# A two-layer attention decoder: who turns the later layer's probabilities and gates

## The chip, the core and the metric

The kernel runs on one core of one Trainium2 chip. The metric is the time of one execution in device microseconds (us), median of the runs. Engines are named TensorE (PE in the profile; its weight loads are PEld), VectorE (DVE), ScalarE (ACT), GpSimd (POOL) and SyncE (SP), which only issues transfers and waits.

## What is computed

A residual stream of 256 tokens x 2048 in float32 goes through two layers. Layer A is latent attention with 16 heads. Layer B, the later one, is dilated sliding-window attention with 16 heads of 128 in three groups (dilation 1, 4, 16), which share one key/value projection. What matters of layer B:

```
u = rms_norm(h) @ w_in                   # queries of 3 groups and a gate
for g, dil in enumerate((1, 4, 16)):
    q = rms_norm(q_all[g]); s = q @ k[g].T * scale + alibi    # within the window
    o[g], lse[g] = softmax(s) @ v[g], log-denominator
o = sum over g of o[g] * softmax(lse)[g]
out = h + (o * silu(gate)) @ w_o
```

## The kernel before

All weights are streamed from device memory once, in steps of 128 x 1024 float32 (512 KB), into a ring of four buffers `raw`. To keep float32 accuracy each step is split in two: ScalarE rounds it to a high half (`highs`, L478), VectorE subtracts to get the low half (`lows`, L794), and TensorE multiplies three of the four products of halves (`three`, `project`, L1271): 12 matmuls of 512 columns for a step.

SyncE issues the weight loads in the order of use (`load`, L363). Load n waits until the low half of step n-3 counted from one is made (semaphore `lo_ready`), so that its place in the ring is free. ScalarE makes the high half of step n once TensorE has used step n-4. So the halves are made about three steps ahead of TensorE.

Layer B goes over 8 pairs of heads, 40 weight steps each, and then the output projection of 32 steps. The order of all work is written out by hand. While TensorE projects pair i (a "quarter" s is two steps, 20 of them in a pair), the attention of pair i-1 is woven in after the quarters. A pair has four units (2 heads x 2 tiles of 128 tokens). A unit u goes through four stages, one a quarter (`b_units`): stage 0 at quarter u+2, the scores (`b_score`, L1514 and L1519), VectorE's mask and maximum (`band_mask`), ScalarE's exponential into `prob`; stage 1 at u+3, VectorE's reciprocal and scaled gate (`b_gates`, `band_gate`, L899, into `og`), and on TensorE `band_turn`, which transposes three 128x128 blocks of `prob` and one of `og` into a PSUM bank (L1303); ScalarE copies them to `probT` (L516); stage 2 at u+4, the product with the values (`band_pv`, L1536 and L1540), in PSUM, and VectorE's product with the turned gate (`band_out`, L904); stage 3 at u+5, the split of the result into halves for the output projection. The last pair's attention stands in the output projection, at the steps of `B_LAST_SLOTS`.

Keys and queries are turned by VectorE in 32x32 blocks: 16 instructions for a tensor, from a block row a to a block column b (`b_blocks`, L1180). A 32x32-block transpose turns each block in place; which partitions a block lies in is changed by reading one quarter of the partitions and writing another. For the third query group 8 of 16 stand in quarter 0 and 8 in quarter 1, with a low half between.

Each engine takes its own instructions in the order written; semaphores are the only ties.

Of the kernel before, what the change touches and what calls it, by code (L numbers as in the profile page):

```python
# [107 lines left out]

def b_round(i, k):

    return i * UNITS + (B_ROUND_0 - UNITS) + k


QUAD = P // 4
# [11 lines left out]


B_LAST_SLOTS = [0, 1, 3, 5, 7, 9, 11, 12, 13]


# [27 lines left out]
def build_program(nc, xT, x_later, x_tok, identity, consts, alibis, gains, w_in, w_pe, w_kv, w_gate_first, w_gate, w_q, w_out_a, w_b, w_out_b, out_tok):  # L158
    ctx = ExitStack()
    with ctx:  # L160
# [19 lines left out]
        gain = sb("gain", [P, N_GAINS])  # L180
        k_per = sb("k_per", [P, TILES, ROPE])
        pe_sq = sb("pe_sq", [P, TILES, ROPE])
        pe_ss = sb("pe_ss", [P, TILES])
# [5 lines left out]
        prob = sb("prob", [P, 2, 512])  # L189
        probT = sb("probT", [P, 512])  # L190
        q_ropes = (qT[:, 2 * 512:3 * 512], v[:, 2 * 512:3 * 512])
        og = sb("og", [P, 2, P])
        out = sb("out", [P, 2, P])
        half = sb("half", [P, 1])
# [73 lines left out]

        pe_T = og[0:ROPE].rearrange("p a k -> p (a k)")

# [41 lines left out]
        blocked = sem("blocked")  # L312
        gained = sem("gained")
        rot_step = sem("rot_step")
        pe_T_ready = sem("pe_T_ready")
# [38 lines left out]
        def _(sp):  # L354
# [110 lines left out]
        def _(act):  # L465
# [323 lines left out]
        def _(dve):  # L789
# [104 lines left out]
            def band_gate(U, u, g, gates_so_far):  # L894
# [265 lines left out]
            def b_gates(i, s):  # L1160

                for stage, u in b_units(s):
                    if stage == 1:
                        U = (i - 1) * UNITS + (B_UNIT_0 + u)
                        unit_den(U, u)
                        band_gate(U, u, gate[:, 0, u % 2, (u // 2) * P:(u // 2 + 1) * P], i + GATE_FILLS)

            def b_blocks(f, k, n):

                buf, x = (B_CHAIN_0 + k) % 2, qT if f in (Q01, Q2GATE) else kT  # L1170
                a, b = n // 4, n % 4
                for first, groups, swap in {Q01: [(0, 2, 0)], K01: [(0, 1, 0), (1, 1, 1)], K2V0: [(0, 1, 1)],
                                            Q2GATE: [(0, 1, 0)]}[f]:
                    at = (first + 2 * (f in (K2V0, Q2GATE))) * 2 * SEQ
                    col = QUAD * (a ^ 2 if swap else a)
                    src = rows[a * QUAD:(a + 1) * QUAD, buf, :, first * 2 * P:(first + groups) * 2 * P]\
                        .rearrange("p t (u d) -> p t u d", d=P)[:, :, :, b * QUAD:(b + 1) * QUAD]
                    dst = x[b * QUAD:(b + 1) * QUAD, at:at + groups * 2 * SEQ]\
                        .rearrange("p (u t d) -> p t u d", t=TILES, d=P)[:, :, :, col:col + QUAD]
                    last = nc.vector.transpose(dst, src)  # L1180
                return last

            def b_attend(i, s, par_before):
                if s == 0:
                    b_rows(i - 1, par_before, 3)
                    dve.wait_ge(rows_ready, i * 4 + B_CHAIN_0)
                if s < 2:
                    for n in range(8 * s, 8 * s + 8):
                        last = b_blocks(Q2GATE, 3, n)
                    if s == 1:  # L1190
                        last.then_inc(blocked, 1)
                for stage, u in b_units(s):
# [69 lines left out]
        def _(pe):  # L1262
# [258 lines left out]

            def band_turn(U, u, rnd):

                pe.wait_ge(prob_ready, U + 1)
                pe.wait_ge(og_ready, U + 1)
                turn_rows(rnd, [(prob[:, u % 2, k * P:(k + 1) * P], k * P) for k in range(BAND // P)]
                          + [(og[:, u % 2], BAND)])

            def band_pv(U, B, u, rnd):

                h, t = u // 2, u % 2
                pe.wait_ge(turn_read, rnd + 1)
                pe.wait_ge(out_made, B)
                both = probT[:, 0:BAND].rearrange("p (a k) -> p a k", a=2)
                for tile in range(TILES):
                    nc.tensor.matmul(pv.rearrange("p (a k) -> p a k", a=2), v[:, tile * 768 + h * P:tile * 768 + (h + 1) * P],  # L1536
                                     both[:, :, tile * P:tile * P + HP], start=tile == 0, stop=False, skip_group_check=True)
                for half, first in ((0, SEQ), (1, HP)):
                    col = t * 768 + (1 + half) * 256 + h * P
                    last = nc.tensor.matmul(pv[:, half * HP:(half + 1) * HP], v[:, col:col + P],  # L1540
                                            probT[:, first:first + HP], start=False, stop=True, skip_group_check=True)
                last.then_inc(pv_ready, 1)

            def b_attend(i, s):
                for stage, u in b_units(s):
                    U = (i - 1) * UNITS + (B_UNIT_0 + u)
                    if stage == 2:
                        band_pv(U, (i - 1) * UNITS + u, u, b_round(i, u))
                    if stage == 1:
                        band_turn(U, u, b_round(i, u))  # L1550
# [150 lines left out]
```

## Time and profile before

| | us |
|---|---|
| median of 3 runs | 1403.69 (1403.6 to 1404.28) |
| the profiled execution | 1404.01 |
| span of its instructions | 1402.2 |
| TensorE busy | 1395.2 |
| VectorE busy | 1046.5 |
| ScalarE busy | 706.6 |

The span is the time from the first to the last instruction in one profiled execution; what lies around it, 1.8 us, is start and end. Busy times are of instructions as recorded; matmuls overlap their neighbours, so that TensorE at 99% need not be at its peak. The chain of waits is followed back from the last instruction, at each step to what released it, and so shows what set the end. The granted clock of TensorE is 1.00 (2.4 GHz) in every stretch.

### The profile page before, as it was taken

How to read it: one execution, taken by the hardware profiler on the slowest of the kernel's cores; microseconds unless marked ns; L12 is line 12 of the kernel's file. 1: busy time of each engine (PE TensorE's matmuls, PEld its weight loads, DVE VectorE, ACT ScalarE, POOL GpSimd, SP SyncE). 2: the span in 40 equal slices, each digit the busy share in tenths (PEclk: the TensorE clock that was granted, in tenths of full speed). 3: DMA queues.
4: the chain of work that ended last, by engine and by line, in shares of the span. 5: the costliest groups of instructions: out<-in, count | busy, mean ns of one | idle time of the engine just before them, and what ended most of it. 6: DMA issues, size and time to landing. Idle time of an engine off the chain costs nothing.

```text
span 1402.2 us, 20187 instructions
## 1 busy us (share of the span) xinstructions
PE 1395.2 (99%) x6648; PEld 1169.4 (83%) x6648; DVE 1046.5 (75%) x1969; ACT 706.6 (50%) x1032; POOL 102.5 (7%) x67
## 2 busy tenths in 40 slices
PE   9999999999999999999999999999999999999999
PEld 6888888888888888888888888888888888888887
DVE  6767767747667868877877877887887788789653
ACT  6555555646544544544544454544454445454442
POOL 0101001000010001000101100101010110010000
PEclk9999999999999999999999999999999999999999
DMA  9653544455556545645654654565556456555544
GB/s 355 232 173 125 166 143 142 147 190 179 183 187 203 191 151 180 205 155 180 182 194 149 197 181 163 183 198 167 166 188 189 159 186 194 160 181 190 171 165 150
DMA packets 71233, 252.49 MB, mean 180 GB/s; under 512 B 7904, under 2 KB 8288, under 8 KB 71136
## 3 DMA queue, kind: packets, MB, share of 16 engines
q1 hardware_dynamic: 70704, 249.95, 54.7%
q10 hardware_dynamic: 432, 1.31, 0.3%
q8 instruction: 53, 0.87, 0.2%
q14 instruction: 44, 0.36, 0.1%
HBM read 249.14 MB, written 2.10 MB: 179 GB/s over the span
## 4 chain that ended last, share of the span: by engine, by line
PE 94%; DVE 2%; issue 2%; ACT 1%; DMA 0%; POOL 0%; SPq 0%; DVEq 0%; POOLq 0%
PE acc L1271 85%; PE turn L1303 1%; PE score L1514 1%; PE pv_bank L1536 1%; PE score L1519 1%; PE pv_bank L1540 1%; DVE qT L1180 1%; PE pv_bank L1315 1%; PE score L1411 1%; PE score L1413 1%; DVE w_lo L794 1%; PE turn L1397 0%; DMA raw<-in_w_in 0%; PE og_bank L1323 0%; POOL rms L426 0%
## 5 line engine op out<-in xcount | busy, mean ns | idle before, releaser
L794 DVE TENSOR_TENSOR w_lo<-raw,w_hi 128x1024 fp32r<-128x1024 f32 x463 | 574.2, 1251 | 205.9 <-ACT w_hi L478 196.9
L478 ACT ACTIVATE w_hi<-raw 128x1024 fp32r<-128x1024 f32 x463 | 482.4, 1050 | 397.2 <-PE acc L1271 386.0
L1271 PE MATMUL acc<-w_hi,xa_hi 128*128 128x512 f32 x956 | 378.7, 396 | 0.6 <-DVE w_lo L794 0.4
L1271 PE MATMUL acc<-w_hi,xa_lo 128*128 128x512 f32 x956 | 372.8, 390 | 0.0
L1271 PE MATMUL acc<-w_lo,xa_hi 128*128 128x512 f32 x956 | 372.2, 389 | 0.0
L1271 PE MATMUL acc<-w_hi,xb_hi 128*128 128x512 f32 (+1 forms) x640 | 249.4, 390 | 0.0
L1271 PE MATMUL acc<-w_hi,xb_lo 128*128 128x512 f32 (+1 forms) x640 | 245.9, 384 | 0.0
L1271 PE MATMUL acc<-w_lo,xb_hi 128*128 128x512 f32 (+1 forms) x640 | 245.5, 384 | 0.0
L1271 PEld LDWEIGHTS acc<-w_hi,xa_lo 128*128 128x128 f32 x956 | 179.4, 188 | 37.9
L1271 PEld LDWEIGHTS acc<-w_hi,xa_hi 128*128 128x128 f32 x956 | 179.6, 188 | 37.5 <-issue 1.3
L1271 PEld LDWEIGHTS acc<-w_lo,xa_hi 128*128 128x128 f32 x956 | 179.7, 188 | 35.3
L426 POOL TENSOR_TENSOR rms<-ms,mhalf 128x4 f32<-128x4 f32 (+2 forms) x50 | 73.2, 1465 | 1050.6 <-DVE ms L850 855.4
L1271 PEld LDWEIGHTS acc<-w_hi,xb_lo 128*128 128x128 f32 x640 | 120.1, 188 | 22.7
L1271 PEld LDWEIGHTS acc<-w_lo,xb_hi 128*128 128x128 f32 x640 | 120.3, 188 | 22.1
L1271 PEld LDWEIGHTS acc<-w_hi,xb_hi 128*128 128x128 f32 x640 | 120.2, 188 | 22.0
L1180 DVE STREAM_TRANSPOSE kT<-rows 32x128 f32<-32x128 f32 x384 | 102.2, 288 | 4.5
L1271 PE MATMUL acc<-w_hi,oT_hi 128*128 128x512 f32 x256 | 102.3, 400 | 0.0
L1271 PE MATMUL acc<-w_hi,oT_lo 128*128 128x512 f32 x256 | 100.0, 391 | 0.0
L1271 PE MATMUL acc<-w_lo,oT_hi 128*128 128x512 f32 x256 | 99.7, 390 | 0.0
L1180 DVE STREAM_TRANSPOSE qT<-rows 32x256 f32<-32x256 f32 (+1 forms) x256 | 94.5, 369 | 4.1
L532 ACT ACTIVATE prob<-prob,top_neg 128x128 f32<-128x128 f32 (+1 forms) x64 | 34.3, 537 | 91.3 <-DVE top_neg L891 63.9
L516 ACT ACTIVATE probT<-turn 128x128 f32<-128x128 f32 (+1 forms) x64 | 29.7, 463 | 76.7 <-PE turn L1303 57.2
(178 smaller groups left out, 1061.4 us busy)
## 6 DMA issues: line engine op xcount, KB each, us to landing
raw<-in_w_b SPq DMA_DIRECT2D x320, 512.0 KB, 3.6
raw<-in_w_out_a SPq DMA_DIRECT2D x32, 512.0 KB, 3.3
raw<-in_w_out_b SPq DMA_DIRECT2D x32, 512.0 KB, 3.3
raw<-in_w_gate SPq DMA_DIRECT2D x30, 512.0 KB, 3.6
raw<-in_w_kv SPq DMA_DIRECT2D x16, 512.0 KB, 4.3
raw<-in_w_in SPq DMA_DIRECT2D x15, 512.0 KB, 6.2
raw<-in_w_q SPq DMA_DIRECT2D x16, 384.0 KB, 3.0
res<-in_x_tok SPq DMA_DIRECT2D x4, 512.0 KB, 7.8
```

What stands on the lines that cost most here:

```text
L426: nc.gpsimd.tensor_tensor(rms[:, 0:width], ms[:, 0:width], mhalf[:, 0:width], ALU.pow)\
L478: nc.scalar.activation(w[0][:, s, 0:width], raw[:, s, 0:width], ACT.Copy).then_inc(hi_ready, 1)
L516: last = nc.scalar.activation(dst, turn[:, 0:width], ACT.Copy)
L532: nc.scalar.activation(prob[:, u % 2, 0:width], prob[:, u % 2, 0:width], ACT.Exp, bias=top_neg[:, u:u + 1], accum_out=den[:, u:u + 1])\
L794: nc.vector.tensor_tensor(w[1][:, s, 0:width], raw[:, s, 0:width], w[0][:, s, 0:width].bitcast(F32), ALU.subtract).then_inc(lo_ready, 1)
L1180: last = nc.vector.transpose(dst, src)
L1271: last = nc.tensor.matmul(out, x(a), y(b), start=start and k == 0, stop=stop and k == 2, **more)
L1303: last = nc.tensor.transpose(turn[:, col:col + P], src, ident[:])
L1315: last = nc.tensor.matmul(pv, probT[:, k * P:(k + 1) * P], val, start=k == 0, stop=k == len(values) - 1)
L1411: nc.tensor.matmul(score[:, 0:n], qT[:, par * 512 + at:par * 512 + at + P], kT[:, k_0 + h * SEQ:k_0 + h * SEQ + n], start=True, stop=False)
L1413: nc.tensor.matmul(score[:, 0:n], q_ropes[par][:, at:at + P], kT[:, k_0 + 512:k_0 + 512 + n], start=False, stop=True).then_inc(scored, 1)
L1514: nc.tensor.matmul(score[:, P:P + SEQ], qT[:, h * SEQ + t * P:h * SEQ + (t + 1) * P], kT[:, h * SEQ:(h + 1) * SEQ], start=True, stop=True)
```

## The change

TensorE turns nothing any more in layer B. For each unit VectorE turns the 128 x 512 of `prob` (384 columns of probabilities and 128 of gate, which now stands behind them in the same buffer) in one instruction, each 32x32 block in its place, into a new buffer `bands`, of which there is one. Then SyncE issues 16 transfers within on-chip memory, one for each pair of block row a and block column b, 32 rows of 512 bytes each, which put the blocks into `probTs`, of which there are two. The semaphore `band_moved` counts the landings. VectorE's turn waits until the transfers of the unit before have landed; TensorE's value product waits for those of its own unit. In SyncE's order the transfers of unit u stand behind the load of step 14 + 2u of a pair (behind loads 12, 14, 16 and 18 in the output projection). The value product and `band_out` read the turned data in pieces of 32 columns. ScalarE's copy from PSUM goes.

Beside this: the later layer's loops of SyncE are written out; `b_blocks` turns two groups in one instruction for the first two key groups too (16 instructions instead of 32); the 16 transposes of the third query group all stand in quarter 0, and ScalarE's gain on it in quarter 1 instead of 2; `k_per`, `pe_sq`, `pe_T`, `og` and `out` lie in buffers that are free at the time.

```
+B_MOVES = [2 * (u + 3) + 2 * RING for u in range(UNITS)]
+B_LAST_MOVES = [B_LAST_SLOTS[u + 3] - 1 + 2 * RING for u in range(UNITS)]
...
+        bands = sb("bands", [P, 512])
...
+        probTs = sb("probTs", [P, 2, 512])
+        probT = probTs[:, 0]
...
+        og = prob[:, :, BAND:BAND + P]
...
# SyncE
-            with sp.Fori(0, PAIRS) as i:
+            def band_move(B, u):
+                sp.wait_ge(band_turned, B + 1)
+                if not isinstance(B, int) or B >= 2:
+                    sp.wait_ge(out_made, B - 1)
+                for a in range(4):
+                    for b in range(4):
+                        sp.dma_start(probTs[b * QUAD:(b + 1) * QUAD, u % 2, a * P:(a + 1) * P],
+                                     bands[a * QUAD:(a + 1) * QUAD, b * P:(b + 1) * P]).then_inc(band_moved, 16)
+            def b_pair(i, attend):
                 for s in range(B_STEPS):
                     load((i, B_STEPS), B_0 + s, w_b[i, s], STEP)
-            with sp.Fori(0, OUT_STEPS // 8) as j:
-                for q in range(8):
-                    load((j, 8), OUT_B_0 + q, w_out_b[j, q], STEP)
+                    if attend and s in B_MOVES:
+                        u = B_MOVES.index(s)
+                        band_move((i - 1) * UNITS + u, u)
...
+            for k in range(OUT_STEPS):
+                load(OUT_B_0 + k, OUT_B_0 + k, w_out_b[k // 8, k % 8], STEP)
+                if k in B_LAST_MOVES:
+                    u = B_LAST_MOVES.index(k)
+                    band_move((PAIRS - 1) * UNITS + u, u)
...
# ScalarE
-                if s == 2:
+                if s == 1:
                     act.wait_ge(blocked, (i - 1) * 4 + 4)
                     gain_of(qT, 2, q_gain)
...
-                    if stage == 1:
-                        if u:
-                            act.wait_ge(out_made, (i - 1) * UNITS + u)
-                        unit_turned(b_round(i, u), u, BAND + P)
...
# VectorE
+            def band_turn(U, B, u):
+                dve.wait_ge(og_ready, U + 1)
+                if not isinstance(B, int) or B:
+                    dve.wait_ge(band_moved, B * BAND_LANDED)
+                nc.vector.transpose(bands[:].rearrange("p (b x j) -> p b x j", b=4, j=QUAD),
+                                    prob[:, u % 2].rearrange("p (x b j) -> p b x j", b=4, j=QUAD))\
+                    .then_inc(band_turned, 1)
...
-                nc.vector.tensor_tensor(out[:, u % 2], pv, probT[:, BAND:BAND + P], ALU.mult).then_inc(out_made, 1)
+                gT = probTs[:, u % 2].rearrange("p (a x i) -> p a x i", a=4, i=QUAD)[:, :, 3]
+                to, o = (x.rearrange("p (a i) -> p a i", a=4) for x in (out[:, u % 2], pv))
+                nc.vector.tensor_tensor(to, o, gT, ALU.mult).then_inc(out_made, 1)
...
                         band_gate(U, u, gate[:, 0, u % 2, (u // 2) * P:(u // 2 + 1) * P], i + GATE_FILLS)
+                        band_turn(U, (i - 1) * UNITS + u, u)
...
-                if s < 2:
-                    for n in range(8 * s, 8 * s + 8):
+                    for n in range(16):
                         last = b_blocks(Q2GATE, 3, n)
...
# TensorE
-            def band_turn(U, u, rnd):
-                pe.wait_ge(prob_ready, U + 1)
-                pe.wait_ge(og_ready, U + 1)
-                turn_rows(rnd, [(prob[:, u % 2, k * P:(k + 1) * P], k * P) for k in range(BAND // P)]
-                          + [(og[:, u % 2], BAND)])
-            def band_pv(U, B, u, rnd):
+            def band_pv(U, B, u):
                 h, t = u // 2, u % 2
-                pe.wait_ge(turn_read, rnd + 1)
+                pe.wait_ge(band_moved, (B + 1) * BAND_LANDED)
                 pe.wait_ge(out_made, B)
-                both = probT[:, 0:BAND].rearrange("p (a k) -> p a k", a=2)
+                pT = probTs[:, u % 2]
...
+                quads = pv.rearrange("p (h a i) -> p h a i", h=2, i=QUAD)
                 for tile in range(TILES):
...
+                    both = bass.AP(pT.tensor, pT.offset + tile * QUAD,
+                                   [parts, [SEQ + QUAD, 2], [P, 2], [1, QUAD]])
+                    nc.tensor.matmul(quads, v[:, tile * 768 + h * P:tile * 768 + (h + 1) * P], both,
+                                     start=tile == 0, stop=False, skip_group_check=True)
...
```

## Rows read from the trace of the kernel before

**Rows 1.** The page, parts 1 and 4: engine, busy us, share of span, instructions; the chain.

```profile
PE 1395.2 (99%) x6648; PEld 1169.4 (83%) x6648; DVE 1046.5 (75%) x1969; ACT 706.6 (50%) x1032; POOL 102.5 (7%) x67
...
PE 94%; DVE 2%; issue 2%; ACT 1%; DMA 0%; POOL 0%; SPq 0%; DVEq 0%; POOLq 0%
PE acc L1271 85%; PE turn L1303 1%; PE score L1514 1%; PE pv_bank L1536 1%; PE score L1519 1%; PE pv_bank L1540 1%; DVE qT L1180 1%; PE pv_bank L1315 1%; PE score L1411 1%; PE score L1413 1%; DVE w_lo L794 1%; PE turn L1397 0%; DMA raw<-in_w_in 0%; PE og_bank L1323 0%; POOL rms L426 0%
```

**Rows 2.** The table of waits: who waited for whom, us in all, times, longest.

```profile
PE score L1514 <- ACT qT L766: 1.5, 3, 0.9
```

**Rows 3.** The chain of waits, 498 to 529 us: start us, us, what.

```profile
498.57 0.44 PE turn L1303 x4
...
499.88 5.47 PE acc L1271 x24
505.36 0.45 PE pv_bank L1536 x4
505.81 0.39 PE pv_bank L1540 x4
506.20 0.58 PE turn L1303 x4
506.78 0.43 PE score L1514 x2
507.21 0.44 PE score L1519 x4
...
513.96 0.45 PE turn L1303 x4
...
527.54 0.45 PE pv_bank L1536 x4
```

**Rows 4.** VectorE in order of time, same pair: start us, us, engine, line, operation.

```profile
497.80 0.29 DVE L899 TENSOR_SCALAR og<-gate,den_inv 128x128 f32<-128x128 f32 x1
498.00 1.22 DVE L794 TENSOR_TENSOR w_lo<-raw,w_hi 128x1024 fp32r<-128x1024 f32 x1
```

**Rows 5.** SyncE's queue in order of time, same pair.

```profile
499.38 0.33 SPq L363 DMA_DIRECT2D raw<-in_w_b  x1
```

**Rows 6.** Groups of ScalarE by form: busy us, mean ns, idle before and its releaser.

```profile
L516 ACT ACTIVATE probT<-turn 128x512 f32<-128x512 f32 x32 | 19.1, 598 | 73.9 <-PE turn L1303 55.3 <-DVE out L904 18.6
```

**Rows 7.** Groups of VectorE by form, line 1180.

```profile
L1180 DVE STREAM_TRANSPOSE kT<-rows 32x128 f32<-32x128 f32 x384 | 102.2, 288 | 4.5
L1180 DVE STREAM_TRANSPOSE qT<-rows 32x256 f32<-32x256 f32 x128 | 55.7, 435 | 2.1
L1180 DVE STREAM_TRANSPOSE qT<-rows 32x128 f32<-32x128 f32 x128 | 38.7, 303 | 2.1
```

**Rows 8.** The attention stretch: us, busy us of each engine, granted clock, DMA share, GB/s.

```profile
498.00:528.00 30.00, 30.00 (x164) 25.79 (x162) 21.31 (x44) 14.15 (x23) 2.55 (x1) 1.00 0.48 158
```

**Rows 9.** The chain of waits in the last pair.

```profile
1309.12 1.23 DVE w_lo L794
...
1346.48 0.45 PE pv_bank L1536 x4
```

**Rows 10.** VectorE in order of time, last pair.

```profile
1319.87 1.22 DVE L794 TENSOR_TENSOR w_lo<-raw,w_hi 128x1024 fp32r<-128x1024 f32 x1
```

**Rows 11.** SyncE's queue in order of time, issues back to back near the start.

```profile
15.22 0.43 SPq L373 DMA_DIRECT2D ident<-in_identity  x1
15.70 0.43 SPq L374 DMA_DIRECT2D phase<-in_consts  x1
16.18 0.43 SPq L376 DMA_DIRECT2D res<-in_x_tok  x1
```

**Rows 12.** DMA issues by what they move: count, KB each, us from issue to landing.

```profile
raw<-in_w_out_b SPq DMA_DIRECT2D x32, 512.0 KB, 3.3
...
raw<-in_w_q SPq DMA_DIRECT2D x16, 384.0 KB, 3.0
```

**Rows 13.** The stretches after the load issued at 505.82.

```profile
506.50:506.80 0.30, 0.30 (x4) 0.30 (x3) 0.30 (x1) 0.00 (x0) 0.30 (x1) 1.00 0.16 27
```

More of the change, by code:

```diff
@@ L180, in build_program @@
         gain = sb("gain", [P, N_GAINS])
-        k_per = sb("k_per", [P, TILES, ROPE])
-        pe_sq = sb("pe_sq", [P, TILES, ROPE])
+        bands = sb("bands", [P, 512])
+        k_per, pe_sq = (bands[:, c * P:(c + 1) * P].rearrange("p (t d) -> p t d", t=TILES) for c in range(2))
         pe_ss = sb("pe_ss", [P, TILES])
@@ L189, in build_program @@
         prob = sb("prob", [P, 2, 512])
-        probT = sb("probT", [P, 512])
+        probTs = sb("probTs", [P, 2, 512])
+        probT = probTs[:, 0]
         q_ropes = (qT[:, 2 * 512:3 * 512], v[:, 2 * 512:3 * 512])
-        og = sb("og", [P, 2, P])
-        out = sb("out", [P, 2, P])
+        og = prob[:, :, BAND:BAND + P]
+        out = gate[:, 1, 0].rearrange("p (a k) -> p a k", a=2)
         half = sb("half", [P, 1])
@@ L267, in h_turned_to @@
             return h_banks[m % 3][:].rearrange("p (c k) -> p c k", c=2)
-        pe_T = og[0:ROPE].rearrange("p a k -> p (a k)")
+        pe_T = bands[0:ROPE, 2 * P:4 * P]
         x_loaded = [sem(f"x_loaded{m}") for m in range(KC // 2)]
@@ L313, in build_program @@
         gained = sem("gained")
+        band_turned = sem("band_turned")
+        band_moved = sem("band_moved")
         rot_step = sem("rot_step")
@@ L397, in _ @@
                     load((j, 8), OUT_A_0 + q, w_out_a[j, q], STEP)
-            with sp.Fori(0, PAIRS) as i:
+            def band_move(B, u):
[7 more added lines that the diff above has]
+            def b_pair(i, attend):
                 for s in range(B_STEPS):
                     load((i, B_STEPS), B_0 + s, w_b[i, s], STEP)
-            with sp.Fori(0, OUT_STEPS // 8) as j:
-                for q in range(8):
-                    load((j, 8), OUT_B_0 + q, w_out_b[j, q], STEP)
+                    if attend and s in B_MOVES:
+                        u = B_MOVES.index(s)
+                        band_move((i - 1) * UNITS + u, u)
+            b_pair(0, False)
+            b_pair(1, True)
+            for i in range(2, PAIRS):
+                b_pair(i, True)
+            for k in range(OUT_STEPS):
[3 more added lines that the diff above has]
+                    band_move((PAIRS - 1) * UNITS + u, u)
             for j in range(OUT_FILLS):
@@ L1171, in b_blocks @@
                 a, b = n // 4, n % 4
[L1172 to L1181, printed above, removed]
+                groups = 2 if f in (Q01, K01) else 1
+                at, swapped = (0, 1) if groups == 2 else (2, 2)
+                if f in (Q01, Q2GATE):
+                    swapped = GROUPS
+                cols = [(at + g) * 2 * SEQ + QUAD * (a ^ 2 if at + g >= swapped else a) for g in range(groups)]
+                src = rows[a * QUAD:(a + 1) * QUAD, buf, :, 0:groups * 2 * P]\
+                    .rearrange("p t (g u d) -> p t g u d", u=2, d=P)[:, :, :, :, b * QUAD:(b + 1) * QUAD]
+                to = x[b * QUAD:(b + 1) * QUAD, cols[0]:cols[0] + QUAD]
+                parts = [list(d) for d in to.ap]
+                dst = bass.AP(to.tensor, to.offset, [parts[0], [P, TILES], [cols[-1] - cols[0] or QUAD, groups],
+                                                    [SEQ, 2], [1, QUAD]])
+                return nc.vector.transpose(dst, src)
             def b_attend(i, s, par_before):
@@ L1186, in b_attend @@
                     dve.wait_ge(rows_ready, i * 4 + B_CHAIN_0)
-                if s < 2:
-                    for n in range(8 * s, 8 * s + 8):
+                    for n in range(16):
                         last = b_blocks(Q2GATE, 3, n)
-                    if s == 1:
-                        last.then_inc(blocked, 1)
+                    last.then_inc(blocked, 1)
                 for stage, u in b_units(s):
@@ L1520, in b_score @@
                 last.then_inc(scored, 1)
-            def band_turn(U, u, rnd):
-                pe.wait_ge(prob_ready, U + 1)
-                pe.wait_ge(og_ready, U + 1)
-                turn_rows(rnd, [(prob[:, u % 2, k * P:(k + 1) * P], k * P) for k in range(BAND // P)]
-                          + [(og[:, u % 2], BAND)])
-            def band_pv(U, B, u, rnd):
+            def band_pv(U, B, u):
                 h, t = u // 2, u % 2
-                pe.wait_ge(turn_read, rnd + 1)
+                pe.wait_ge(band_moved, (B + 1) * BAND_LANDED)
                 pe.wait_ge(out_made, B)
-                both = probT[:, 0:BAND].rearrange("p (a k) -> p a k", a=2)
+                pT = probTs[:, u % 2]
+                parts = [list(d) for d in pT.ap][0]
+                tiles = pT.rearrange("p (a x i) -> p a x i", a=4, i=QUAD)
+                quads = pv.rearrange("p (h a i) -> p h a i", h=2, i=QUAD)
                 for tile in range(TILES):
-                    nc.tensor.matmul(pv.rearrange("p (a k) -> p a k", a=2), v[:, tile * 768 + h * P:tile * 768 + (h + 1) * P],
-                                     both[:, :, tile * P:tile * P + HP], start=tile == 0, stop=False, skip_group_check=True)
-                for half, first in ((0, SEQ), (1, HP)):
+                    both = bass.AP(pT.tensor, pT.offset + tile * QUAD,
+                                   [parts, [SEQ + QUAD, 2], [P, 2], [1, QUAD]])
+                    nc.tensor.matmul(quads, v[:, tile * 768 + h * P:tile * 768 + (h + 1) * P], both,
+                                     start=tile == 0, stop=False, skip_group_check=True)
+                for half, x in ((0, 2), (1, 0)):
                     col = t * 768 + (1 + half) * 256 + h * P
-                    last = nc.tensor.matmul(pv[:, half * HP:(half + 1) * HP], v[:, col:col + P],
-                                            probT[:, first:first + HP], start=False, stop=True, skip_group_check=True)
+                    last = nc.tensor.matmul(quads[:, half], v[:, col:col + P], tiles[:, 2 * half:2 * half + 2, x],
+                                            start=False, stop=True, skip_group_check=True)
                 last.then_inc(pv_ready, 1)
@@ L1547, in b_attend @@
                     if stage == 2:
[L1548 to L1550 removed]
+                        band_pv(U, (i - 1) * UNITS + u, u)
                     if stage == 0:
```

3 lines of the change are left out of this document (1 added, 2 removed).

## Prediction, made before the result was known

> **What bounds the kernel now.** I read the page first. TensorE is busy for 1395.2 of 1402.2 us and the chain that ended last is 94% TensorE, 85% the projections of L1271; VectorE is at 75% [rows 1]. What can be gained is therefore TensorE time alone, and everything else costs nothing until TensorE has to wait for it. The table of waits says how near that is: TensorE waited 1.5 us in all for the scores' operands, 0.9 at the longest [rows 2].
>
> Then I read the chain of waits over one pair of the later layer, 498 to 529 us [rows 3]. It shows the rhythm: 24 projection matmuls (two weight steps) 5.47, the value product of one head tile ("unit") 0.45 + 0.39, the turning of a later unit 0.44 to 0.58, the scores of a still later one 0.43 + 0.44. A slot is 7.6 to 7.8 us with the turning and 5.47 + 0.84 + 0.87 = 7.18 without. VectorE and SyncE come after, in order of time: VectorE scales the gate of unit 0 at 497.80 and from 498.00 works on the low half of the next weight step (1.22 us) [rows 4]; SyncE waits for such a low half before each weight load and issues the load 0.16 us after it (499.22 to 499.38) [rows 4, 5].
>
> **What is removed.** In each of 32 units four turnings on TensorE: 0.44, 0.58, 0.45 and, in the fourth slot of a pair, the same 0.45 again [rows 3], mean 0.48, so 32 x 0.48 = 15.4 us off the bounding engine. ScalarE loses 32 copies of 0.60 (19.1 us) [rows 6]; this stands in no piece of the chain shown, so that is worth nothing. The value product now reads its moving operand in pieces of 32 columns. The trace has none such; it streams as many columns as before. I take no change; a gain has no source, and doubling its 0.84 would cost 27 us, an end that I hold very unlikely.
>
> **What VectorE gets.** A transpose of 32x128 takes 0.303, one of 32x256 0.435 [rows 7]: 0.13 per 128 elements a lane, so one of 128x512 is about 0.303 + 3 x 0.13 = 0.70. Bounds: 4 x 0.13 = 0.53 without any fixed part, 4 x 0.303 = 1.2 if it were like four instructions. It stands in front of a low half, 32 x 0.70 = 22 us in all. Against it, the keys' 32 small transposes per pair become 16 of double size: 32 x 0.29 - 16 x 0.435 = 2.3 us per pair less. VectorE was idle for 8.7 of the 30 us from 498 to 528 [rows 8], which covers both. The 16 query transposes now come in one slot, which puts one low half 2.4 us later, with the weights prepared three steps (8 us) ahead: nothing. It also takes a low half (1.23) out of the path to the last pair's first scores, where the chain does go through these transposes [rows 9]; I count 1 us gained, of at most the 1.5 of [rows 2].
>
> **What SyncE gets: the term that decides.** After a certain weight load, SyncE waits for the turned blocks and issues 16 transfers of 32 rows x 512 B, 512 issues in all. Their cost isn't bytes. Where issues stand back to back with no wait between, one takes 0.43 and they start 0.48 apart, for the 64, 192 and 512 KB of identity, tables and rows of x alike (15.22, 15.70, 16.18); the load issued after a wait takes 0.33 [rows 5, 11]. No row has an issue of 32 rows instead of 128. Bounds: a quarter of 0.48, 0.12, if the issue's time were all per row; 0.48 if it is per instruction. Since an eightfold change in bytes does not move it, I take 0.48.
>
> The Trainium skill, "DMA: Bandwidth & Descriptors" (under Why a DMA increments its semaphore by 16 and not by 1, where it compares descriptor generation), gives 512 cycles of the sequencer for each DMA instruction on generations before the newest, data movement apart; at the 1.2 GHz that "Advanced Engine Details and Errata" (Clock Domains) gives for SyncE that is an estimate of 0.43. The trace has 0.43 for its issues, all of 128 rows; that an issue of 32 rows is no cheaper no row shows. By that rule the sum below stands; by a cost per row the first rival would.
>
> The landing of the last one, counted from its issue: weight loads of 384 KB land after 3.0 and of 512 KB after 3.3 [rows 12], 0.3 per 128 KB, so 16 KB about 3.0 - 0.9 = 2.1. The data of the load issued at 505.82 is just beginning to move in the stretch from 506.5 on (DMA share 0.16), 0.7 to 1.0 after the issue [rows 13], so not under 0.9. The source is on the chip here; I take 1.8, bounds 0.9 and 2.8.
>
> The wait chain is closed on itself, because there is a single buffer of turned blocks. VectorE may turn unit u+1 only when unit u's 16 transfers have landed; behind this wait stand its own low half, for which SyncE's next load waits, and behind that load stand the next 16 transfers. One turn of this circle:
> turn 0.70 + low half 1.23 + to SyncE 0.16 + load issue 0.36 + 15 x 0.48 = 7.20 + landing 1.80 = 11.45 us.
> TensorE's slot is 7.18, so the circle, not TensorE, sets the pace while four units pass. It starts at 498.00, where the turn of unit 0 will stand. Unit 0 lands at 509.45, while TensorE wants it at 504.9 (its slot from 499.88 less the turning of 0.44, then 5.47): a stall of 4.6. Units 1, 2 and 3 land at 520.9, 532.4 and 543.8; TensorE stalls 4.3 each for the first two and 5.1 for the last, which has no scores in its slot. The value product of unit 3 begins at 543.8 instead of 527.54 [rows 3]: 16.26 us later, the turnings' gain already in it. Seven pairs: 113.8. The last pair stands in the output projection, its circle starting at 1319.87 [rows 10], its last value product at 1346.48 [rows 9]; it ends at 1319.87 + 4 x 11.45 = 1365.67, 19.2 later. After unit 3 nothing is given back, since TensorE was the bound already. SyncE's loops over the pairs are also written out as straight code; if a fetch of code came late it would eat into the weights' lead, which is three steps, so nothing. Weights do not run out: SyncE gets two loads in per circle and TensorE uses two steps.
>
> Sum: 113.8 + 19.2 - 1.0 = +132 us on the profiled execution's 1404.01, that is 1536; the median shown (1403.69) is 0.3 below it, which I neglect.
>
> The other ends of the terms: landing 0.9 gives a circle of 10.55 and 1507; landing 2.8 one of 12.45 and 1568. Issues at 0.36 apart (the 0.33 of the row after a wait) give 9.65: 7 x 9.06 + 12.0 = +75, 1478.
>
> **Rivals.**
> 1. *Small transfers issue cheaply (slot stays TensorE's).* The circle loses its hold when 4 circles fit in the 29.5 us between turn and last value product, 7.4 each: that is at issues 0.21 apart. At 0.12 it is 11.45 - 15 x 0.36 = 6.05, under the 6.9 from 498.00 to 504.9, there is no stall, and the 15.4 + 1 us are gained: 1388. For it: all issues in the trace have 128 rows. Against: bytes per row from 512 to 4096 change nothing. Chance 0.10.
> 2. *Issues 0.36 apart*: 1478, as above; between this and 0.48 lies the rest of its range. For it, every issue in the middle of the kernel takes 0.33. Against, each stands behind a wait, and the 16 don't. Chance 0.13.
> 3. *The clock falls in the stalls.* The granted clock is 1.00 in all the stretch [rows 8], and the longest wait of TensorE that I found in the later layer is the 0.9 of [rows 2], so no row shows what 4 us do. If it were granted half (1.2 of 2.4 GHz) through the four units, a slot would be 2 x 7.18 = 14.4 > 11.45, and TensorE sets the pace again: unit 3 at 509.45 + 3 x 14.4 - 1.7 = 550.9, 23 us per pair, some 1590. A shorter fall is paid out of the next stall and costs nothing. Chance 0.08.
> 4. *The value product slows on its pieces*: inside the circle it is hidden in the stalls too, at most 0.84 after each unit 3, 7 us: inside the range.
>
> The Trainium skill, "TensorE: Matmul & The Clock Gate" (Why this matters for your kernels), warns of idle gaps between bursts of matmuls, after which the clock is back at half. By that rule rival 3 is what the stalls bring; no run yet shows it.
>
> **How the numbers follow.** Forecast 0.65 (its range 1507 to 1568), rivals 0.10, 0.13, 0.08, and 0.04 for what I haven't seen. The likeliest is 1536; the range reaches to 1475 below and 1580 above, leaving out rival 1 and most of 3. Faster by over 0.2% (what a measurement of this kernel can tell from none) 0.11; same 0.02; slower 0.87.
>
> **What would show it.** In the changed profile: SyncE issuing 16 transfers in a row 0.48 apart; VectorE idle before its 128x512 transpose (0.70), released by a transfer; TensorE idle before the first value matmul of each unit, some 4 to 5 us, released by a transfer too; the span of a unit in the attention stretches near 11.5 and in the rest of a pair unchanged; no turn rows at L1303 from the later layer. It is wrong if the issues are below 0.21 apart, if the stalls are named for weights, or if the granted clock drops below 1.00 outside the start.

## The result and the profile after

The changed kernel takes 1631.11 us (median of 4 runs) against 1403.78: a ratio of 1.162, 95% interval 1.161 to 1.164. It is slower by 227 us; the forecast was slower by 132, with 1580 as the end of the range. The direction and the circle of waits held; the price of an issue, and that a fall of the clock would cost nothing, did not.

The page of the changed kernel, parts 1, 2 and 4, against [rows 1]:

```profile
span 1628.6 us, 19232 instructions
...
PE 1464.5 (90%) x6520; PEld 1216.9 (75%) x6520; DVE 1059.2 (65%) x1873; ACT 688.8 (42%) x1000; POOL 101.6 (6%) x67
...
PEclk9999999999998899799989988987997899899889
...
PE 64%; SPq 18%; DVE 6%; DMA 5%; issue 4%; ACT 1%; POOL 0%; DVEq 0%; ACTq 0%; POOLq 0%
PE acc L1306 60%; SPq L412 17%; DVE w_lo L817 4%; DMA probTs<-bands 3%; DMA raw<-in_w_in 1%; ACT w_hi L505 1%; DVE qT L1218 1%; PE pv_bank L1569 1%; PE pv_bank L1350 1%; PE score L1446 1%; PE score L1448 1%; SPq L369 1%; DVE prob L909 0%; PE turn L1432 0%; PE pv_bank L1573 0%
```

TensorE's share of the chain fell from 94% to 64%, and 17% of it is now SyncE's line L412, the 16 transfers. The granted clock (PEclk, in tenths; 9 stands for 0.90 and more) is at 7 or 8 in many slices of the later layer; these hold the stretches where TensorE waits.

The table of waits (in all, times, longest) and VectorE's new instruction, of which [rows 7] gave the estimate of 0.70:

```profile
PE pv_bank L1569 <- DMA probTs<-bands: 158.7, 32, 8.4
DVE bands L929 <- DMA probTs<-bands: 130.5, 24, 7.0
```

```profile
L929 DVE STREAM_TRANSPOSE bands<-prob 128x512 f32<-128x512 f32 x32 | 22.8, 711 | 131.3 <-DMA probTs<-bands 130.5
```

TensorE waits in all 32 units for a landing, VectorE before 24 of its 32 turns, those behind a first unit. The turn takes 0.71.

The chain of waits over the first unit of the same pair as in [rows 3 to 5] (start us, us, what):

```profile
498.17 0.71 DVE bands L929
498.88 1.12 DVE w_lo L817
...
500.02 0.33 SPq L369
...
500.39 0.60 SPq L412
...
501.03 0.58 SPq L412
...
509.26 0.59 SPq L412
...
509.89 1.80 DMA probTs<-bands
...
511.79 0.71 DVE bands L929
```

This is the forecast's circle, link by link: turn 0.71, low half 1.12, load issue, then 16 issues, then a landing of 1.80, then the next turn, 13.62 us after the last (511.79 - 498.17). One link is wrong: the issues start 0.63 apart (500.39, 501.03), not 0.48. Issues of 16 KB landed after 1.8 us:

```profile
probTs<-bands SPq DMA_DIRECT2D x512, 16.0 KB, 1.8
```

The end of the same pair, and what follows:

```profile
550.62 1.77 DMA probTs<-bands
...
552.43 1.22 PE pv_bank L1569 x4
553.65 0.75 PE pv_bank L1573 x4
554.40 83.20 PE acc L1306 x360
637.60 0.43 PE score L1549 x2
```

The last value product starts at 552.43; before it was 527.54 [rows 3]. Then it takes 1.22 + 0.75 instead of 0.45 + 0.39, and the 360 projection matmuls behind it 83.20; before they took 81.67. That is 2.7 us more. The stretches show why (us, busy us of TensorE, its weight loads, VectorE, ScalarE, GpSimd, granted clock, DMA share, GB/s):

```profile
508.00:511.00 3.00, 0.00 (x0) 0.00 (x0) 0.00 (x0) 0.00 (x0) 0.00 (x0) 0.77 0.11 26
511.00:515.00 4.00, 3.26 (x13) 3.09 (x14) 2.11 (x3) 0.00 (x0) 0.00 (x0) 0.50 0.53 157
516.00:518.00 2.00, 2.00 (x9) 1.60 (x9) 1.92 (x6) 0.91 (x3) 0.00 (x0) 0.88 0.37 125
554.00:560.00 6.00, 6.00 (x21) 4.84 (x21) 4.73 (x9) 1.26 (x2) 1.64 (x1) 0.71 0.23 88
560.00:570.00 10.00, 10.00 (x46) 8.29 (x45) 9.46 (x14) 3.56 (x4) 0.00 (x0) 1.00 0.60 201
```

TensorE idles from 504.97 to 511.74. While it does, the granted clock goes from 1.00 (504 to 508) to 0.50 (1.2 of 2.4 GHz), stays there for the first matmuls after the wait, and is back at 1.00 some us later. The Trainium skill ("TensorE: Matmul & The Clock Gate", Why this matters for your kernels) warns that idle gaps between bursts of matmuls bring the clock back to half; the trace agrees, with 0.50 behind a wait of 6.8 us.

### The profile page after: what moved, and what is told of

It reads as the page before. It is cut to its first block, busy times and chain, and to the rows that moved or that the text cites. A ratio compares the mean times of both kernels' runs of the same rounds, so it can differ in the third digit from the quotient of the medians.

```text
span 1628.6 us, 19232 instructions
## 1 busy us (share of the span) xinstructions
PE 1464.5 (90%) x6520; PEld 1216.9 (75%) x6520; DVE 1059.2 (65%) x1873; ACT 688.8 (42%) x1000; POOL 101.6 (6%) x67
## 4 chain that ended last, share of the span: by engine, by line
PE 64%; SPq 18%; DVE 6%; DMA 5%; issue 4%; ACT 1%; POOL 0%; DVEq 0%; ACTq 0%; POOLq 0%
PE acc L1306 60%; SPq L412 17%; DVE w_lo L817 4%; DMA probTs<-bands 3%; DMA raw<-in_w_in 1%; ACT w_hi L505 1%; DVE qT L1218 1%; PE pv_bank L1569 1%; PE pv_bank L1350 1%; PE score L1446 1%; PE score L1448 1%; SPq L369 1%; DVE prob L909 0%; PE turn L1432 0%; PE pv_bank L1573 0%
## 5 line engine op out<-in xcount | busy, mean ns | idle before, releaser
L1306 PE MATMUL acc<-w_hi,xa_hi 128*128 128x512 f32 x956 | 395.6, 414 | 0.1
L1306 PE MATMUL acc<-w_lo,xa_hi 128*128 128x512 f32 x956 | 385.9, 404 | 0.0
L1306 PE MATMUL acc<-w_hi,xa_lo 128*128 128x512 f32 x956 | 384.3, 402 | 0.0
L1306 PEld LDWEIGHTS acc<-w_hi,xa_hi 128*128 128x128 f32 x956 | 190.4, 199 | 39.6 <-DVE rows L1036 0.3
L1306 PEld LDWEIGHTS acc<-w_hi,xa_lo 128*128 128x128 f32 x956 | 187.8, 196 | 41.3
L1306 PEld LDWEIGHTS acc<-w_lo,xa_hi 128*128 128x128 f32 x956 | 189.1, 198 | 38.3
L1569 PE MATMUL pv_bank<-probTs,v 128*128 128x128 f32 x128 | 36.8, 438 | 158.7 <-DMA probTs<-bands 158.7
L1569 PEld LDWEIGHTS pv_bank<-probTs,v 128*128 128x128 f32 x128 | 27.7, 302 | 172.2 <-DMA probTs<-bands 172.2
L929 DVE STREAM_TRANSPOSE bands<-prob 128x512 f32<-128x512 f32 x32 | 22.8, 711 | 131.3 <-DMA probTs<-bands 130.5
```

The costliest lines, as they stand in the source:

```text
L929: nc.vector.transpose(bands[:].rearrange("p (b x j) -> p b x j", b=4, j=QUAD), prob[:, u % 2].rearrange("p (x b j) -> p b x j", b=4, j=QUAD))\
L1306: last = nc.tensor.matmul(out, x(a), y(b), start=start and k == 0, stop=stop and k == 2, **more)
L1569: nc.tensor.matmul(quads, v[:, tile * 768 + h * P:tile * 768 + (h + 1) * P], both, start=tile == 0, stop=False, skip_group_check=True)
```

## The experiments

I read two lengths from each trace. *Inside*: from the turn of a pair's first unit to the start of its last value product (before, from the low half at 498.00 in [rows 4]: 29.4, in the last pair 26.5). *Outside*: from there to the next pair's first turn, or to the end of the kernel (before, by the same mark: 88.4 to 89.1 in the first six pairs, 84.3 in the seventh, 55.9 at the end). In the changed kernel inside is 54.3 to 55.0; outside is 90.8 to 91.9, 88.1 and 57.8. Over all eight pairs inside grew by 204 us and outside by 22.

The runs e1, e4, e5, e6, e7, e10, e12 and e17 were executed once, the others four or ten times.

**e1: what an issue costs.** TensorE turns, as in e2 below, and SyncE issues dummy transfers, of another form in each pair. No engine that computes waits for them; SyncE itself waits for those of the unit before, 4.1 us in all.

```diff
+ pair 1, 8: probTs[32 rows] <- ident[32 rows x 512 B]     pair 2: the same from device memory
+ pair 3: 128 rows x 128 B, on-chip                        pair 5: the same from device memory
+ pair 4: 32 rows x 16 B   pair 6: 1 row x 512 B   pair 7: 32 rows x 128 B, partitions kept
```

> TensorE turns again, as before the change; the other edits stay. In addition SyncE issues the 16 transfers of each unit as dummies that nobody waits for, back to back, and each pair has another form: pair 1 and 8 as in the change (on-chip source, 32 rows x 512 B, partitions crossed), pair 2 the same from device memory, pair 3 on-chip source with 128 rows x 128 B, pair 4 on-chip with 32 rows x 16 B, pair 5 device memory with 128 rows x 128 B, pair 6 on-chip with 1 row x 512 B, pair 7 on-chip with 32 rows x 128 B and no crossing of partitions. Theory A (an on-chip source makes the issue dear): 0.63 us apart in pairs 1, 3, 4, 6, 7, 8 and 0.48 in 2 and 5. Theory B (rows or bytes): pairs 4 and 6 are cheaper, pair 3 differs from pair 1. Theory C (straight code or the place in the kernel): 0.63 in all. The kernel's time by all of them about 1403, since nobody waits for the dummies; if SyncE's time were itself the limit of the weights it would be above 1410.

Measured: 1478.73. The issue itself (duration ns min/median/max), pair 1 and pair 2:

```profile
L419 SPq DMA_DIRECT2D probTs<-ident x64: 512/590/1014, 499.7 to 544.7; - x64
```

```profile
L421 SPq DMA_DIRECT2D probTs<-in_identity x64: 320/421/1407, 629.7 to 663.7; - x64
```

The other on-chip forms have medians of 601 (128 rows), 590 (16 bytes), 589 (one row) and 591 (partitions kept); device memory with 128 rows 432. Sixteen in a row took, undisturbed, 10.0 us from the on-chip source and 7.3 from device memory, 0.63 and 0.46 each. So theory A: rows, bytes and crossed partitions count for next to nothing, the on-chip source for 0.17 us. My rows at 0.48 [rows 11] all had a source in device memory, and I took the rows' count for the open question when it was the source.

No computing engine waits for the dummies, and still the run is 75 us above the kernel before, and 68 above e2, which is the same kernel without them. Two waits from the table of waits of e1 (in all, times, longest):

```profile
ACT w_hi L528 <- DMA raw<-in_w_b: 129.1, 50, 9.1
PE acc L1330 <- DVE w_lo L844: 41.4, 14, 4.4
```

ScalarE waits for weights, which it does not in e2, and TensorE for low halves, since SyncE, busy for 10 us per unit of 7.2 to 7.8 us, issues weight loads late. Outside grew against the kernel before by 12 to 13 us with any on-chip form (9 in the last pair), by nothing with pair 2's form and by 4 with pair 5's; about 2 each of pairs 3 and 5 are there in e2 too. "Weights do not run out" in my forecast is true only because the circle stalls TensorE more than the late loads would.

**e2: only the turning undone.**

```diff
-  dve: transpose prob -> bands; sp: 16 transfers     +  pe: 4 transposes; act: copy to probT
   merged key transposes, query transposes in one quarter, SyncE written out, shared buffers: stay
```

> Only the turning is undone: TensorE turns probabilities and gates again and ScalarE copies them; SyncE's written-out loops, the merged key transposes, the query transposes in one quarter and the buffers in shared places stay. If the transfers are the whole cause: 1402 to 1404, up to 1.5 below the kernel before (the scores' waits). If the other edits have a part in the 227 us: clearly above 1404.

Measured: 1410.51, ratio 1.005 (1.003 to 1.007): the other edits cost some 6.5 us. TensorE's wait, and the chain before it:

```profile
PE acc L1312 <- DVE w_lo L826: 5.0, 2, 2.6
```

```profile
836.25 2.04 issue
...
839.22 0.30 DVE qT L1224
...
844.30 1.24 DVE w_lo L826
```

Where VectorE's loop goes round there is a gap of 2.04 that nothing in the profile explains but its own queue. The kernel before has two such gaps as well (4.8 us in its table of waits, TensorE waiting 0.4). New is what follows: 16 query transposes stand in front of the low half of 844.30, which now is late. Two such places, 5.0 us.

**e8: also the query transposes split again,** 8 in quarter 0 and 8 in quarter 1, ScalarE's gain in quarter 2.

```diff
-  for n in range(16): b_blocks(Q2GATE, 3, n)
+  if s < 2: for n in range(8 * s, 8 * s + 8): b_blocks(Q2GATE, 3, n)
```

> TensorE turns as before the change, and also the 16 query transposes stand in two quarters again, ScalarE's gain in quarter 2; what is left of the other edits is the merged key transposes, SyncE's written-out loops and the shared buffers. The kernel with only the turning undone took 1410.5, its TensorE waiting 5.0 us for low halves right behind the loops' ends of VectorE. Theory (the 16 transposes in one quarter make that low half late where VectorE's code comes late too): 1403 to 1404. Rival (the written-out loops or the merged transposes cost it): 1409 to 1411.

Measured: 1405.58, ratio 1.0012 (1.0003 to 1.0022). So 4.9 us are the query transposes in one quarter; I had counted this edit as a gain of 1. The 1.9 us that stay stand outside in pairs 3 and 5, where scores now wait for ScalarE's gain (3.8 us in all, before 1.5); which of the edits left does that is not shown. In the changed kernel the query transposes do not show: TensorE waits 0.3 us there for low halves.

**e3 and e4: the same bytes in 4 and 8 transfers.** They leave out the crossing of partitions, so that the values are not those of the reference.

```diff
-  16 x (32 rows x 512 B)
+  e3:  4 x (32 rows x 2 KB), block rows kept      e4:  8 x (32 rows x 1 KB), block rows kept
```

> The same bytes in 4 transfers of 32 rows x 2 KB in place of 16 of 512 B; the blocks stay in their partitions, so the crossing of partitions is left out. Theory (the circle is set by the count of issues, 0.63 each): it shrinks from 13.6 by 12 x 0.63 to 6.0 us, below TensorE's slot of 7.18, no stall is left, and the time is 1404 - 15.4 - 1 = 1387 to 1389, a little more if the value product pays for its pieces of 32 columns. Rival (the bytes or the rows' transport set the circle): it stays near 1631. Rival (the landing, not the issue): it stays above 1500.

> The same bytes in 8 transfers of 32 rows x 1 KB, blocks left in their partitions. By the count of issues: circle 13.6 - 8 x 0.63 = 8.5, stalls of about 1.5 us at each unit, 4.8 later per pair (last pair 7.5), 1403.7 + 7 x 4.8 + 7.5 - 1 = 1444, and the granted clock at 1.00 all through. By bytes: 1631. If the clock falls though the stalls are short, above 1460.

Measured: e3 1403.07, ratio 0.9996 (0.9987 to 1.0006); e4 1460.23. The count of issues sets the time, not the bytes: inside 54.3, 34.7 and 28.2 us with 16, 8 and 4. The 34.7 of e4 is about 4 x 8.6, the circle worked out from 0.63. Its time is 16 above what I wrote: the mean clock is 0.984 and not 1.00, stalls are up to 4.7, and outside is 10 us longer over all pairs (88.8 to 90.9, 86.6, 59.0), of which I had counted none.

But e3 shows that nearly nothing of the 15.4 us comes in even so. What TensorE still waits, and two of its slots at full clock:

```profile
PE pv_bank L1568 <- DMA probTs<-bands: 7.9, 8, 2.4
```

```profile
514.37 5.50 PE acc L1305 x24
519.87 0.45 PE pv_bank L1568 x4
520.31 0.39 PE pv_bank L1572 x4
520.71 5.55 PE acc L1305 x24
```

The value product on pieces of 32 columns takes the 0.45 + 0.39 of [rows 3]: free. Of the 15.4, 7.9 go to waits of up to 2.4 (in the chain a 64 KB transfer landed after 2.4, not 1.8); 4.6 of them stand in the last pair, whose inside was 26.5 before and not 29.4. About 2 go to the first matmuls after a wait (0.71 instead of 0.45, 8 times), about 2.2 to an outside longer by 0.3 a pair. That leaves 3; the span is shorter by 1.3, and the difference isn't traced.

**e5: the clock.** 20 unused matmuls before each wait for a landing.

```diff
+  for _ in range(20): matmul(turn, xa_hi[:, 0], xa_hi[:, 0:2])
   pe.wait_ge(band_moved, ...)
```

> The changed kernel, and TensorE computes 20 unused matmuls of 512 columns (4.5 us, into an empty bank) before it waits for a unit's landing, so that it is hardly idle in the stalls. Read from the traces: turn to last value product takes 54.3 us per pair in the changed kernel, and from there to the next pair's first turn 2.7 us more than before, 2.0 at the end. Theory (these 21 us are the lower clock after the last stall; the circle itself does not depend on TensorE): the granted clock stays at 1.00, the 54.3 us stay within 0.3, and the 2.7 us fall to 0.5, so 1631 - 17 to 21 = about 1612. Rival (the 2.7 us are the value product's pieces or late weights): 1631 stays. Rival (the clock makes the circle too): the 54.3 us fall too, below 1600.

Measured: 1623.82, mean clock 0.986: 7 us less where I expected 17 to 21. Outside fell to within 0.7 us of the kernel before in five of seven pairs (88.8 three times, 89.2, 85.0), so 2 to 3 us per pair are indeed the clock. It stayed longer by 3.1 (92.2), 1.9 (90.4) and, at the end, 2.6 (58.5); before the first and the last of these the value product still took 1.22, the time of the low clock, instead of 0.71. In all 12 of the 22 us came back. Inside rose to 54.5 to 56.0: in two units the unused matmuls held up the value product by 1.5 and 1.0 us, the rest isn't traced. That inside did not fall shows that the clock is hidden there, as the forecast said of a short fall.

**e6: the transfers in front of the weight load.**

```diff
-  load(s); band_move(u)
+  band_move(u); load(s)
```

> The changed kernel with the 16 transfers of a unit in front of the weight load instead of behind it. The circle then has no low half (1.12) and no load issue (0.37) in it: 13.6 - 1.5 = 12.1 us, four of them 6.0 us less per pair, 1631 - 8 x 6.0 = 1583. If the circle is another (SyncE's whole time per unit, 16 issues and two loads, 10.9): the same 12.1, since that is less. If the wait on the low half is not in the circle: 1631.

Measured: 1582.75, as expected; inside 48.1 to 48.7. The low half and the load issue were in the circle, with just their durations.

**e7, e9, e10: two queues.** ScalarE issues a part of the transfers right behind its wait for the turned blocks; in e9 and e10 SyncE's stand in front of the load.

```diff
-  sp: 16 transfers
+  sp: 8, act: 8 (e7, e9)      sp: 10, act: 6 (e10)
```

> The changed kernel with 8 of the 16 transfers issued by SyncE and 8 by ScalarE, right behind its wait for the turned blocks. Theory (each engine's sequencer pays 0.63 per issue, side by side): the circle is that of 8 issues, 8.5 to 9 us, the time that of the kernel with 8 transfers, 1460, some more since ScalarE's high halves wait 5 us. Rival (one generator of descriptors serves both, one issue at a time): the circle stays at 13.6 and the time at 1631 or above.

> 8 transfers from SyncE, in front of the weight load, and 8 from ScalarE. Circle by SyncE: turn 0.71 + 0.2 + 8 issues 5.0 + landing 1.8 less the last issue, about 7.2 us against TensorE's slot of 7.18; the first unit is wanted 6.9 after its turn. By that: a stall of 0.3 and then next to none, 1404 - 15.4 + 5 (query transposes in one quarter) + 5 = 1398 to 1402. If ScalarE's 5 us of issues per unit hold up its exponentials and high halves (two queues behind the load took 9.5 per circle instead of 8.5): a circle of about 8.2, 1404 + 8 x (4 x 8.2 - 29.5) - 1 = 1430.

> 10 transfers from SyncE in front of the load, 6 from ScalarE. If SyncE's issues set the circle: 7.2 + 2 x 0.63 = 8.4 us, 1404 + 8 x (4 x 8.4 - 29.5) = 1437, slower than with 8 and 8. If ScalarE's issues set it: 1.3 us less per circle than with 8 and 8.

Measured: 1486.10, 1485.77 (ratio 1.058, 1.056 to 1.060) and 1457.66. Two queues issue side by side, but moving SyncE's in front gained nothing, where I had expected 1398 to 1430: the other branch set the circle. ScalarE in e9:

```profile
498.23 5.36 ACTq L363 DMA_DIRECT2D probTs<-bands  x8
503.64 0.62 ACT L563 ACTIVATE prob<-prob,top_neg 128x384 f32<-128x384 f32 x1 [6.96 <-issue]
```

It issues for 5.4 us and only then computes the next unit's exponential, for which VectorE's next turn waits. Two issues fewer on ScalarE gave 28 us, though SyncE had two more.

**e11, e13 to e17: three queues,** GpSimd with a semaphore of its own.

```diff
+  e11: sp 7, act 4, pool 5, pool's behind its own chain step of the quarter
+  e13: sp 5, act 4, pool 7, in front of it        e14: and query transposes split
+  e15: sp 7, act 4, pool 5, in front of it        e16: and split        e17: 8, 4, 4 and split
```

> 7 transfers from SyncE in front of the load, 4 from ScalarE, 5 from GpSimd with a semaphore of its own. Circle by SyncE: 0.71 + 0.2 + 7 x 0.63 + 1.2 = 6.5 us, below the slot and below the 6.9 in which the first unit is wanted: no stalls, 1404 - 15.4 + 0 to 7 for the other edits = 1389 to 1396, faster than both kernels. If GpSimd's issues cost more than 1 us each or land later: circle 0.9 + 5 + 2 = 8 or more, 1425 and above.

> 5 transfers from SyncE in front of the load, 4 from ScalarE, 7 from GpSimd; GpSimd's for a unit now stand in front of its own chain step of that quarter, behind which its first unit's stood 8 us late before. GpSimd starts an issue every 0.49 us. Circle 0.71 + 0.25 + 6 x 0.49 + 2.0 = 5.9 us, the longest branch of the three, below both 7.18 and 6.9: no stall, the clock at 1.00, 1404 - 15.4 = 1389 and up to 7 more for the other edits (5 for the query transposes in one quarter). That would settle that issue and landing were the whole loss. If it stays above 1404, something besides them eats the 15.4, and the kernel with 4 transfers (1403) already showed it.

> The same, with the query transposes in two quarters again and ScalarE's gain in quarter 2. With TensorE turning, that edit was worth 1410.5 - 1405.6 = 4.9 us. If it is worth the same here, 5 us below the run beside it, about 1386 to 1391; if that loss was hidden there (in the kernel with 4 transfers TensorE waited only 0.5 us for low halves), within 1 us of it.

> 7 transfers from SyncE in front of the load, 4 from ScalarE, 5 from GpSimd in front of its chain step: the shares of the run with three queues that took 1465, whose 6.4 us stalls stood at first units alone, and the order of the one that took 1424. There GpSimd's last transfers landed 3.5 us after their issue, and I put that on the weight load that SyncE issued in the middle of them; now the load comes 3.3 instead of 1.8 us after... SyncE's 7 issues, when GpSimd's 5 are out. If that is it: landings 2.0 after the last issue at 502.4, so 504.6 where 504.6 to 504.9 is wanted, circle 7.1 against 7.18, and 1404 - 15.4 + 5 (query transposes) = 1392 to 1397. If three queues at once slow the landings by themselves: 1415 to 1425 again.

> The same with the query transposes in two quarters: 3 us below the run beside it, as 1420.7 was below 1423.6.

> 8 from SyncE, 4 from ScalarE, 4 from GpSimd, else as the last. If SyncE's issues set the circle: 0.63 more per unit, 7.7, +0.5 x 32 = 16 us above the run with 7. If the load in the middle sets the landings: the same or less.

GpSimd's loop over the pairs is written out as straight code in all six.

Measured: 1464.89, then 1423.60, 1420.72, 1421.36, 1422.10 and 1420.78. In e11 GpSimd's first transfers stand behind its slow power step (start us, us):

```profile
504.34 2.55 POOL L458 TENSOR_TENSOR rms<-ms,mhalf 128x8 f32<-128x8 f32 x1 [26.00 <-DVE ms L894]
506.84 2.64 POOL L364 DMA_DIRECT2D probTs<-bands  x5
511.74 2.44 POOL L364 DMA_DIRECT2D probTs<-bands  x5 [2.25 <-DVE bands L951]
```

The turned blocks were there at 498.6; from 504.34 on it computes, and issues at 506.84. Put in front with the same shares (e15), that wait is gone and some 44 us with it. But no kernel came below 1420. In e14:

```profile
498.91 3.62 POOL L364 DMA_DIRECT2D probTs<-bands  x7 [20.54 <-DVE bands L951]
...
501.81 4.24 SPq L377 DMA_DIRECT2D raw<-in_w_b  x2
...
506.09 0.68 PE L1594 MATMUL pv_bank<-probTs,v 128*128 128x128 f32 x4 [1.40 <-issue]
```

SyncE's weight load stands in the middle (501.81). The last of seven was issued by 502.5, and TensorE started at 506.09, not at 504.5. In e13 and e14 GpSimd's semaphore has its full count last in 27 of 32 units, 3.3 us (median) after its last issue began; the counts of the six before were reached after 2.0 to 2.1. That is the late landing which holds TensorE there. With SyncE's load behind seven issues instead of five (e15) it is 2.9 us, and in 31 of 32 units the semaphore of the other two queues is the last. This helped the first unit of that pair (504.88), not the total: TensorE waits before value products for 23.4 us in e14 and 22.9 in e15, against 7.9 with four transfers (e3), most of what lies between 1421 and the 1388 hoped for. The landings by queue (SyncE, GpSimd, ScalarE) in e15:

```profile
probTs<-bands SPq DMA_DIRECT2D x224, 16.0 KB, 2.3
probTs<-bands POOLq DMA_DIRECT2D x160, 16.0 KB, 2.2
...
probTs<-bands ACTq DMA_DIRECT2D x128, 16.0 KB, 2.5
```

They are above the 1.8 of the changed kernel, but the third queue need not be the reason. With two queues the medians are 2.3 and 2.4 in e7 and 1.8 and 1.8 in e9; and in the changed kernel, with one, the first three of the 16 landed after 3.0, 2.6 and 2.2 (medians of 32 units), all from the fourth on after 1.8. What these early ones share is a weight load still on its way; in e15's first unit it was so from 497.43 to 502.07, with the transfers issued from 498.64 on. Three queues put most of their issues into that time. How much is the load and how much the third queue, no run separates, and why GpSimd's last landing is late stays open too. My expectation, between 1386 and 1397, was wrong three times (e13, e14, e15), by 24 to 35 us. Also e16, expected 3 us below e15, was 0.7 above it, and e17, 16 above it if SyncE's issues set the pace, was 0.6 below.

**e12: by way of device memory.** One store of the turned blocks, four loads with the partitions crossed.

```diff
-  16 x probTs <- bands
+  turned_hbm <- bands; wait; 4 x probTs[32 rows] <- turned_hbm, in front of the load
```

> 5 transfers instead of 16: one stores the turned blocks to device memory, four bring them back with the partitions crossed, in front of the weight load; VectorE waits only for the store. Issues 0.6 + 4 x 0.46 = 2.4 us in place of 10; but two landings one behind the other, 4.2 (256 KB to device memory, as the output's) and 2.4: 9 us from turn to value product instead of 13.6, 6.9 wanted. A stall of 2 us at the first unit, then little, since turns no longer wait for landings: 1404 - 15.4 + 28 = 1416 +- 10. Rival (the landings too are paid in every unit): 1460.

Measured: 1439.12, between the 1416 expected and the rival's 1460; inside 31.4 to 33.9. Five issues in place of 16, and two landings one behind the other:

```profile
turned_hbm<-bands SPq DMA_DIRECT2D x32, 256.0 KB, 4.5
probTs<-turned_hbm SPq DMA_DIRECT2D x128, 64.0 KB, 2.0
```

Nothing here beats the kernel before.

## Why the prediction was wrong

- *TensorE is the bound, and only its time can be gained.* Right.
- *Turn 0.70, low half 1.23, landing 1.80.* 0.71, 1.12 and 1.80: right. e6 took the low half and the load out of the circle, and just that came back.
- *Issues 0.48 apart.* **This step failed.** They are 0.63 apart, because their source is on the chip (e1). 15 x 0.15 = 2.25 us per circle, four circles in a pair, eight pairs: 72 us of the 95 that are missing. The rows behind 0.48 were all reads of device memory; I varied bytes and doubted rows, and never asked about the source. The forecast's ends (0.12 and 0.48) did not hold the truth, and rival 2 lay on the wrong side.
- *The single buffer closes the circle at 11.45.* The form was right (e4 and e6 scale with it), at 13.6. No run gives the turned blocks a second buffer; SyncE's own time per unit, 16 issues and two loads, some 10.9 us, would then still be above the slot of 7.18.
- *After unit 3 nothing is lost.* This step failed too, by 22 us: 20 in seven stretches and 1.9 at the end, of which e5 gives back 12 with the clock; the other 10 are argued from the one stretch shown, where 2.7 us stand in matmuls at a low clock. I had the clock as a rival that sets the pace inside, and wrote that a shorter fall costs nothing. It does cost in the last stall of a pair, which no further stall pays for. A clock below 1.00 was on my list of signs that the forecast is wrong, and it came.
- *A gain of 1 from the query transposes.* With TensorE turning it was a loss of 4.9 (e2, e8); in the changed kernel neither shows.
- *Weights do not run out.* In the changed kernel right, but not for the reason given: e1 loses 68 us against e2 by SyncE's time alone.
- *Value product on pieces.* No price, as taken (e3).

The forecast's 133 us inside, 72 for the issues and 22 outside make the 227 measured.

## What to carry to other kernels

Count the transfers, not their bytes, and price an issue from a row with the same source and destination; where only rows of another kind are there, that difference is a bound to leave open upward too. Then follow the wait that gives the buffer back: a single buffer puts issue, landing and whatever stands between them in both queues into one period, and that period has to be below the slot of the bounding engine. A small stall in front of a long dense stretch costs more than its length.

## What the runs showed of the hardware that I had not expected

- An issue on SyncE takes 0.59 us (0.63 apart) with an on-chip source, whether 1, 32 or 128 rows, 16 bytes or 512 a row, and 0.42 to 0.43 (0.46 apart) with one in device memory, for 32 and for 128 rows (e1). The Trainium skill's 512 cycles for a DMA instruction ("DMA: Bandwidth & Descriptors", Why a DMA increments its semaphore by 16 and not by 1), from which my estimate of 0.43 came, fit the second and not the first.
- SyncE and ScalarE issue side by side (5.0 and 5.4 us for eight each, started together, e9); GpSimd needs 2.4 to 2.6 us for five (e11) and 3.6 for seven (e13).
- Of 16 transfers of 16 KB behind a weight load the first three land after 3.0, 2.6 and 2.2 us, the others after 1.8 (medians in the changed kernel). With three queues GpSimd's last one lands after 3.3 (e13, e14).
